# The head sums of a recurrent layer as four 64x64 quarter products in place of one product with a block matrix of ones

## The reference

```
def _rwkv7_branch(...):
    ...                                   # r, k, v from the projection, with the token before mixed in
    kk = (k * k_k).reshape(B, T, N_HEADS_B, RWKV_HEAD)
    kk = kk / jnp.maximum(jnp.linalg.norm(kk, axis=-1, keepdims=True), 1e-12)      # sum 1: of squares of kk
    k = k * (1.0 + (aa - 1.0) * k_a)
    ...
    o = _rwkv7_scan(rh, hs(decay), kh, vh, kk, hs(aa))
    mu = jnp.mean(o, axis=-1, keepdims=True)
    var = jnp.mean(jnp.square(o - mu), axis=-1, keepdims=True)                     # sum 2: of squares of o
    o = ((o - mu) * lax.rsqrt(var + GN_EPS)).reshape(B, T, D_B)
    o = o * ln_x_w + ln_x_b
    bonus = jnp.sum(rh * kh * r_k_h, axis=-1, keepdims=True) * vh
    o = (o + bonus.reshape(B, T, D_B)) * g
    return o @ w_proj_b
```

## Time and profile before

| | |
|---|---|
| median of 3 runs | 3597.92 us (3595.99 to 3604.17) |
| the profiled execution's own time | 3598.56 us |
| its span | 3596.8 us |
| mean granted TensorE clock | 0.995 of full speed |
| the recurrence's four rounds | from about 2530 us to 3081 us of the span |
| TensorE (PE) busy | 3554.1 us, 99% |
| VectorE (DVE) busy | 1813.5 us, 50% |
| ScalarE (ACT) busy | 1279.8 us, 36% |

### The profile page before, as it was taken

How to read it: one execution, slowest core, us unless ns; L and a number is a source line. 1 busy time by engine, 2 the same in 40 slices (tenths; PEclk the granted TensorE clock), 3 DMA queues, 4 the chain that set the end, 5 groups by cost and what they waited for, 6 DMA issues and landing times.

```text
span 3596.8 us, 50918 instructions
## 1 busy us (share of the span) xinstructions
PE 3554.1 (99%) x21862; PEld 2912.6 (81%) x21862; DVE 1813.5 (50%) x2482; ACT 1279.8 (36%) x1967; POOL 333.6 (9%) x319
## 2 busy tenths in 40 slices
PE   9999999999999999999999999999999999999999
PEld 8887888877788887888888888888887777788887
DVE  5445434454543445543344544335667767655344
ACT  5444322344422233332234443224433433543222
POOL 2021101100110111110010211002000000000000
PEclk9999999999999999999999999999999999899999
DMA  7213333321333233232332123233322312533232
GB/s 231 77 59 94 95 99 94 100 66 58 94 99 101 88 103 88 94 102 89 103 94 83 53 94 94 90 103 95 110 59 81 84 53 77 166 115 105 89 96 80
DMA packets 325571, 337.67 MB, mean 94 GB/s; under 512 B 12256, under 2 KB 306402, under 8 KB 325090
## 3 DMA queue, kind: packets, MB, share of 16 engines
q1 hardware_dynamic: 325058, 334.33, 30.2%
q10 hardware_dynamic: 288, 0.09, 0.0%
HBM read 319.69 MB, written 14.68 MB: 93 GB/s over the span
## 4 chain that ended last, share of the span: by engine, by line
PE 94%; DVE 4%; ACT 1%; issue 1%; POOL 0%; DMA 0%; DVEq 0%; SPq 0%; POOLq 0%
PE P L97 92%; PE P L100 2%; DVE lo L118 0%; DVE sP L148 0%; DVE sA L118 0%; DVE rw_S L118 0%; DVE ds L126 0%; POOL sP L161 0%; DVE x L118 0%; DVE rw_r L126 0%; DVE rw_k L126 0%; DMA memn<-in_mem_dram 0%; POOL sA L161 0%; DVE rw_S L126 0%; DVE rw_kk L118 0%
## 5 line engine op out<-in xcount | busy, mean ns | idle before, releaser
L97 PE MATMUL P<-aH,lo 128*128 128x512 f32 x2840 | 1131.9, 399 | 4.2 <-DVE q L126 1.4
L97 PE MATMUL P<-aH,hi 128*128 128x512 f32 x2840 | 1106.9, 390 | 0.0
L97 PE MATMUL P<-aL,hi 128*128 128x512 f32 x2840 | 1106.3, 390 | 0.0
L111 ACT ACTIVATE hi<-raw 128x1024 fp32r<-128x1024 f32 (+2 forms) x607 | 610.4, 1006 | 1038.5 <-PE P L97 1033.0
L118 DVE TENSOR_TENSOR lo<-raw,hi 128x1024 fp32r<-128x1024 f32 (+2 forms) x607 | 747.7, 1248 | 246.7 <-ACT hi L111 246.6
L97 PEld LDWEIGHTS P<-aH,lo 128*128 128x128 f32 x2840 | 533.6, 188 | 131.7 <-issue 17.0
L97 PEld LDWEIGHTS P<-aH,hi 128*128 128x128 f32 x2840 | 533.1, 188 | 112.7
L97 PEld LDWEIGHTS P<-aL,hi 128*128 128x128 f32 x2840 | 533.8, 188 | 111.7 <-issue 5.5
L97 PE MATMUL P<-bH,lo 128*128 128x512 f32 x832 | 325.5, 391 | 2.5 <-DVE hold L118 2.5
L97 PE MATMUL P<-bH,hi 128*128 128x512 f32 x832 | 324.2, 390 | 0.0
L97 PE MATMUL P<-bL,hi 128*128 128x512 f32 x832 | 324.2, 390 | 0.0
(11 more groups left out here) (325 smaller groups left out, 4185.1 us busy)
## 6 DMA issues: line engine op xcount, KB each, us to landing
raw<-in_w_ffn_in_dram SPq DMA_DIRECT2D x176, 512.0 KB, 3.6
raw<-in_w_in_dram SPq DMA_DIRECT2D x163, 512.0 KB, 3.9
raw<-in_w_ffn_out_dram SPq DMA_DIRECT2D x96, 384.0 KB, 3.1
raw<-in_w_ffn_dram SPq DMA_DIRECT2D x62, 512.0 KB, 3.8
raw<-in_w_o_dram SPq DMA_DIRECT2D x26, 512.0 KB, 3.5
raw<-in_w_mem_kv_dram SPq DMA_DIRECT2D x16, 512.0 KB, 6.4
raw<-in_w_ffn_out_dram SPq DMA_DIRECT2D x16, 512.0 KB, 3.5
held_dram<-hold SPq DMA_DIRECT2D x24, 256.0 KB, 2.1
```

The costliest lines, as they stand in the source:

```text
L97: return self.e.matmul(out, l, r, start=start, stop=stop, skip_group_check=skip) if self.e else Nothing()
L111: return self.e.activation(out, in_, func, scale=scale)
```

## The change

Both sums are made of four products of 64x64 by 256 columns, one in each quarter of the array, in place of one of 128x128 by 512 columns. The first 256 columns of the squares are summed into bank `3u`, the others into bank `3u+1`. For the second half the column half of the array is exchanged, so the sum of head 0 would land in the partitions of head 1. To put that right, ScalarE writes the squares of the second half with the heads exchanged, in two instructions of 64 partitions where one of 128 was. Both readers read two banks. Bank `3u+1` is taken before the products and given free by the reader of the sums. Three estimates of the planner are changed; the merged order of the steps comes out the same.

```diff
@@ pair_steps
-    out += [..., vec("rw_unit", dve=0.5, gap=0.8, gives=[("kk2", p)])]
+    out += [..., vec("rw_unit", dve=0.5, gap=1.25, gives=[("kk2", p)])]
...
-    out += [Step("rw_square", p, u, pe=0.9, needs=[("kk2", p)]), ...
+    out += [Step("rw_square", p, u, pe=0.5, needs=[("kk2", p)]), ...
@@ tensor_program
+    def head_sums(u, src):
+        ones = K.const(K_BONES)
+        for y in range(2):
+            for h in range(2):
+                r, o = slice(64 * h, 64 * h + 64), slice(64 * (h ^ y), 64 * (h ^ y) + 64)
+                t = e.mm(P[o, 3 * u + y, 0:256], ones[r, r], src(r, y), True, True, True)
+        return t
+
     def rw_square(p, u):
+        s = m["rw"][u]["S0"]
         e.wait_ge(*S.rw_act[u].at((p, "kk2")))
-        take(3 * u)
-        e.mm(bank(3 * u), K.const(K_BONES), m["rw"][u]["S0"], True, True).then_inc(*S.rw_product[u].up((p, "kk2")))
-        rw_free(u, 0, S.rw_dve[u], (p, "kk_norm"))
+        take(3 * u, 3 * u + 1)
+        head_sums(u, lambda r, y: s[r, 256 * y:256 * y + 256]).then_inc(*S.rw_product[u].up((p, "kk2")))
+        for j in range(2):
+            rw_free(u, j, S.rw_dve[u], (p, "kk_norm"))
...
     def rw_var(p, u):
         e.wait_ge(*S.rw_act[u].at((p, "squared")))
-        take(3 * u)
-        e.mm(bank(3 * u), K.const(K_BONES), m["rw"][u]["k"], True, True).then_inc(*S.rw_product[u].up((p, "var")))
-        rw_free(u, 0, S.rw_act[u], (p, "var_read"))
+        take(3 * u, 3 * u + 1)
+        k = m["rw"][u]["k"].rearrange("p (q x f) -> p x q f", x=2, f=64)
+        head_sums(u, lambda r, y: k[r, y]).then_inc(*S.rw_product[u].up((p, "var")))
+        for j in range(2):
+            rw_free(u, j, S.rw_act[u], (p, "var_read"))
@@ scalar_program
     def rw_unit(p, u):
...
-        e.act(A["S0"], A["kk"], ACT.Square).then_inc(*S.rw_act[u].up((p, "kk2")))
+        e.act(A["S0"][:, 0:256], A["kk"][:, 0:256], ACT.Square)
+        for h in range(2):
+            t = e.act(A["S0"][64 * h:64 * h + 64, 256:512], A["kk"][64 - 64 * h:128 - 64 * h, 256:512], ACT.Square)
+        t.then_inc(*S.rw_act[u].up((p, "kk2")))
...
     def rw_out(p, u):
...
-            e.act(even(A["k"], x), P[:, 3 * u + 1 + x, 0:256].rearrange("p (q f) -> p q f", f=64), ACT.Square
-                  ).then_inc(*mine.up((p, ("half squared", "squared")[x])))
+            o = P[:, 3 * u + 1 + x, 0:256].rearrange("p (q f) -> p q f", f=64)
+            if x:
+                for h in range(2):
+                    t = e.act(even(A["k"], x)[64 * h:64 * h + 64], o[64 - 64 * h:128 - 64 * h], ACT.Square)
+            else:
+                t = e.act(even(A["k"], x), o, ACT.Square)
+            t.then_inc(*mine.up((p, ("half squared", "squared")[x])))
@@ rw_root (ScalarE), rw_norm (VectorE): read P[:, 3 * u:3 * u + 2, 0:256] in place of bank(3 * u)
```

More of the change, by code:

```diff
@@ L409, in pair_steps @@
     out = [Step("rw_begin", p, u)] + first[:6] + [Step("lora_tail", p, u, act=0.3, dve=0.3)] + first[6:]
-    out += [vec("rw_lora", pe=2.6, dve=1.75, wait=1.9), vec("rw_unit", dve=0.5, gap=0.8, gives=[("kk2", p)])]
+    out += [vec("rw_lora", pe=2.6, dve=1.75, wait=1.9), vec("rw_unit", dve=0.5, gap=1.25, gives=[("kk2", p)])]
     out += proj("v", 2, 2)
-    out += [Step("rw_square", p, u, pe=0.9, needs=[("kk2", p)]), vec("rw_norm", dve=0.68, gap=2.6, gives=[("inverse", p)])]
+    out += [Step("rw_square", p, u, pe=0.5, needs=[("kk2", p)]), vec("rw_norm", dve=0.68, gap=2.6, gives=[("inverse", p)])]
     out += proj("r", 0, 1)
@@ L431, in pair_steps @@
                                                                         lat=0.0 if ck < 7 else 0.5)]
-    out += [vec("rw_out", dve=0.7, gap=0.5, hold=True), Step("rw_var", p, u, pe=0.9, lat=0.7), Step("rw_root", p, u, lat=1.5),
+    out += [vec("rw_out", dve=0.7, gap=0.5, hold=True), Step("rw_var", p, u, pe=0.5, lat=0.7), Step("rw_root", p, u, lat=1.5),
             vec("rw_end", dve=2.3, gives=[("end", p)])]
@@ L1550, in rw_root @@
         e.wait_ge(*S.rw_product[u].at((p, "var")))
-        e.act(A["k"], bank(3 * u), ACT.Ln, 1.0 / 64, eps(2)).then_inc(*mine.up((p, "var_read")))
+        e.act(A["k"].rearrange("p (q x f) -> p x q f", x=2, f=64), P[:, 3 * u:3 * u + 2, 0:256].rearrange("p x (q f) -> p x q f", f=64), ACT.Ln,
+              1.0 / 64, eps(2)).then_inc(*mine.up((p, "var_read")))
         e.wait_ge(*mine.now())
@@ L1934, in rw_norm @@
         e.wait_ge(*S.rw_product[u].at((p, "kk2")))
-        e.ts(A["S1"], bank(3 * u), 1e-24, None, ALU.max).then_inc(*mine.up((p, "kk_norm")))
+        e.ts(A["S1"].rearrange("p (y f) -> p y f", y=2), P[:, 3 * u:3 * u + 2, 0:256], 1e-24, None, ALU.max).then_inc(*mine.up((p, "kk_norm")))
     def rw_key(p, u):
```

## The result

| | before | after |
|---|---|---|
| median | 3597.75 us (7 runs, 3595.99 to 3604.17) | 3610.44 us (7 runs, 3605.11 to 3613.84) |
| ratio, 95% interval | | 1.0028 [1.0016, 1.0041] |
| the profiled execution | 3598.56 us, span 3596.8, mean clock 0.995 | 3609.75 us, span 3608.0, mean clock 0.993 |

The changed kernel is slower, by 0.28%. The forecast was 3602 us and "the same"; the time lies above the range's upper end of 3608. A second measurement on another chip gave 3608.36 us, ratio 1.0029 [1.0019, 1.0039]. So some 4 us of the difference were forecast, and 7 to 8 were not (of the medians 12.7 and 11.5 us, of the span of the profiled execution 11.2).

A forecast was written before the change was run, and what follows sets the result against it. TensorE, busy 99% of the span, was taken to bound the kernel. Squares +5.0, ends of rounds 2 and 3 +0.3, round 1 -0.5, round 4 -0.55 gave +4.25 us on 3598.56: 3602.8, as median 3602; 8-in-10 range 3597.5 to 3608.

The forecast's parts named there:

- the same: Whole kernel: 0.12% slower, inside the 0.2% (7.2 us) that measurement can tell from no change; chance 0.79.
- The squares: Squares of kk, four rounds: r projection waits for VectorE's clamp to free bank 3u+1, 1.25 us later each, +5.0 us.
- 0.22 us a set: Head sums: four quarter products of 256 columns run beside one another, 0.22 us a set, two sets a sum.
- +0.15 a round for rounds 2 and 3: Ends of rounds 2 and 3: k projection waits for Ln, using up the sums' savings; +0.15 us each, bounds 0 and +0.3.
- the gain of 0.5 in round 1: End of round 1: sums running at half clock take half as long in quarters; -0.5 us, bounds 0 and -0.9.
- Round 4's gain, -0.55: End of round 4: even pair's sum at half clock 0.85 us less, started 0.3 later; -0.55 us, bounds 0 and -0.9.
- The spacing of the half-width squares: Round ends: ScalarE's extra square of the second half delays the product by one spacing, up to 0.33 us.
- the fall of the clock: Rival at the squares: clock falls in the new pause, 1.7 us a time, 6.8 for the four, 3609 us; chance 0.11.

The follow-up runs named there:

- experiment 1: Kernel before with its full-width sums and squares, only taking bank 3u+1 too and freeing it after the clamp or Ln: 3601.72 us against 3597.47, ratio 1.0015.
- second pair of traces: Both kernels measured and traced once more, no edit: before 3598.79 us, ratio to itself 1.0003; after 3608.36 us, ratio 1.0029.
- experiment 3: Changed kernel with the squares of kk as in the kernel before, so only the ends of the rounds are changed: 3595.67 us, ratio 0.9993.
- experiment 9: Changed kernel with both pairs' squares 21 matmuls earlier, VectorE's clamp right behind: 3598.46 us, ratio 0.9994; likewise with the kernel before's ends: 3588.83 us, ratio 0.9974.
- experiment 2: Changed kernel with the ends of the rounds as in the kernel before, so only the squares of kk are changed: 3596.79 us, ratio 0.9996.
- experiment 6: Kernel before with 64 more 8x8 products in TensorE's first wait, moving its later code: 3591.53 us against 3596.89, ratio 0.9990.
- experiment 8: Changed kernel with the second half of the outputs squared in one instruction of 128 partitions, heads not exchanged there: 3595.18 us, ratio 0.9998.
- experiment 4: Changed kernel with full-width products on constants added in TensorE's two waits at a round's end: 3604.16 us, ratio 1.0018.
- experiment 7: Kernel before with 6 small products added in the first wait and 6 ahead of each end wait: 3609.15 us, 1.0025; with 3 at the ends: 3596.58 us, 0.9992.

## Why the prediction was right and where it wasn't

**The squares: right, in place, size and cause.** Forecast +1.25 us and an idle time of 1.6 to 1.8; measured +1.24 and 1.67, four times. That the clamp decides whatever the product costs is shown by experiment 1. That quarters of 256 columns run four abreast was forecast at 0.22 us a set, measured at about 0.21. The Trainium skill, "TensorEngine Tiling (Array Packing)", "Gotcha 1: PSUM Pressure", would have had the two row halves take turns at one bank; the sixteen records in 1.09 us say otherwise, and the measurement decides.

**The end of a round: the step that failed is "+0.15 a round for rounds 2 and 3", and the gain of 0.5 in round 1.** Measured between the last quarter product and the next squares: +2.2 and +2.8 us, and +1.3 (+0.5 in the second pair of traces). Round 4's gain, -0.55, came out at -0.4, but not as worked out: the even sum ran at full clock, and the clock fell at 3089.64, as the odd one had begun. Two sizes were off, and one thing was left out.
- The spacing of the half-width squares. I took 0.33 us as a mean over three full-width ones. That mean hid two kinds, 0.28 and 0.38: the kernel before's four squares of round 2 begin 0.46, 0.28 and 0.47 us after one another, the short distance being that from the even pair's last to the odd pair's first. In the changed kernel the distances are 0.46, 0.39, 0.40, 0.41 and 0.39, and a square of 64 partitions is as long as one of 128 (0.38). Six ended 2.43 us after the first began, not 2.2, and Ln with them: 2809.69 at the end of round 2, 3.0 us behind the last quarter product, where I had 2.4 to 2.6. By itself, at full clock, that would make the end 0.6 us longer and not 0.15 (2.95 + 0.06 + 0.34 us behind the last record of the quarter products at 2806.74, against 2.75 behind that at 2802.28 before; an estimate from these rows).
- The clock. I had weighed the fall of the clock only for the new rest at the squares, with 0.11. There it never fell, in any of the five traces that have the rest of 1.67 us, nor behind the 0.98 us of experiment 1. It fell at the ends: with the exchanged squares at all twelve ends of rounds 1 to 3 in four traces (the changed kernel twice, experiment 3, and 9 with the changed ends; two of the twelve lie in a long stretch, at the others the clock was at 0.50 for 3.4 or 6.8 us), with the old ends at 4 of 18 (before twice, experiments 1, 2, 6 and 9), with the ends of experiment 8 at 1 of 3, with the fuller ends of experiment 4 at none; with the small products of experiment 7 at three of three and one of three. Dense work behind an end then runs at half rate. What one fall costs the old ends show, which are otherwise alike: 30.6 to 30.8 us from the last quarter product to the next squares with a fall, 29.0 without (both traces of the kernel before, experiments 2 and 6). With the 0.6 us above that makes the +2.2 of round 2.
- Round 1 was to gain since its sums ran at half clock. It lost instead: the clock fell again, in the first trace for 6.8 us (2666.39 to 2673.22), over the sums and the first 4 us of the projection behind them, in the second for 3.4 (2668.56 to 2671.97). Another 0.6 us were lost in its steps, 15.3 us in place of 14.7 in both traces, with a rest for `issue` of 0.4 us in them.

**Left out altogether: that the kernel before carries a long stretch at half clock, worth 5 to 8 us.** I had read its last row as a fact of round 4. It is there in four of the thirteen other traces: before again and experiment 1 (round 4, behind rests for `issue` of 0.9 to 1.7 us), and the changed kernel's two (round 3). In the changed kernel's round 3 it costs about what it cost in round 4 before (steps of 19.8 us in place of 14.1, and of 20.3 in place of 15.0), so it isn't the change's price; but every variant that lost it looked better by more than its edit was worth, and experiments 2 and 3, the two halves of the change, added up to -2.5 us where the whole is +11 to +13. The 15.0 us are those of experiment 9; the rests ahead of it are another 2.4. At equal mean clock the changed kernel stays 7 to 8 us above the kernel before on the same chip: 3607.3 us (two runs) against 3599.0 (five) at 0.994, 3603.0 (two) against 3595.8 (four) at 0.996. So of the 11 to 13 us some 4 go with the clock, an estimate from few runs.

**What stays open.** What starts the long stretch. A rest for `issue` stands ahead of it each time, yet experiment 8 has the same rest at the same matmul and no stretch, experiment 4 has two, of 0.78 and 0.76 us, ahead of round 3's steps and none, and experiment 7 put the code within 6 records of where the changed kernel has it and got neither. Why the clock falls at one end and not at another of the same kind (4 of 18) isn't shown either. The split of the unforeseen 7 us follows from the traces of both kernels, and each experiment has one trace; none shows it whole.

## What to carry to other kernels

A smaller product is worth what the engine doesn't have to wait for afterwards: a second output bank is a second release to wait for, and it stands with whichever engine reads last. Read the granted clock of every stretch beside its time before the halves of a change are added up; here one half-clock stretch, which an edit without work took away, was larger than either half. And where the engine waits already, count the instructions of the engine that it waits for, not their elements.

## What the runs showed of the hardware that was not expected

- **Code comes in pieces, and a piece can be late.** The page of the kernel before has a queue of its own for it (packets, MB, share of 16 engines):

```profile
q8 instruction: 172, 2.82, 0.3%
```

  2.82 MB in 172 packets are 16 KB each, for 21862 matmul records: 127 a packet, with their weight loads, if the queue is TensorE's, as the count suggests. The rests for `issue` of over 0.15 us, 40 in the fourteen traces, stand near records 13511, 13638, 15413, 15541, 17318, 17445, 18967, 19092, 19220 and 19347 of the stream, multiples of 127 apart to within 7 (a few records can be missing from a trace). And each of the 40 ends 1.2 to 1.5 us after a packet of this queue has landed; in the kernel before, for one, the packet lands at 3054.69 and the rest ends at 3056.05. So these are waits for code, as far as times can show it. All but one, which stands right behind them, come in the small products, which get through 127 records in the shortest time.
- **ScalarE takes as long for 64 partitions as for 128**: 0.38 us for 256 columns out of PSUM either way. Behind a square of 64 partitions the next one began 0.39 us later at the least, where one of 128 let the other pair's begin after 0.28 (and its own pair's after 0.38). All those of 64 partitions exchange the heads too, so the width isn't shown apart from that.
